# Gathered expert rows taken whole: 8 KB in one gather and one vector operation of 2048 columns

## What is computed

```python
q = (xb @ w_q).reshape(T, PEER_HEADS, 2, PEER_HALF)
sc = jnp.einsum('thcd,hckd->thck', q, sub_keys)
s1, i1 = lax.top_k(sc[:, :, 0], PEER_TOPK)
s2, i2 = lax.top_k(sc[:, :, 1], PEER_TOPK)
...
idx = e1 * PEER_N_KEYS + e2                 # 8 heads x 16 picks of 16384 experts
g = jax.nn.softmax(best.astype(jnp.float32), axis=-1)
u_sel = jnp.take(u_tab, idx, axis=0)        # rows of 2048
act = jax.nn.gelu(jnp.einsum('td,thkd->thk', xb, u_sel))
v_sel = jnp.take(v_tab, idx, axis=0)
return jnp.einsum('thk,thkd->td', g.astype(act.dtype) * act, v_sel)
```

## Time and profile before

| | |
|---|---|
| time, median of 3 runs | 1738.58 us (1735.13 to 1742.35) |
| time of the profiled execution | 1741.15 us |
| its span, first to last instruction | 1739.4 us |
| granted TensorE clock | 0.996 |
| busy: TensorE 1696.9, VectorE 1453.8, ScalarE 983.1, GpSimd 546.7 us | 98, 84, 57, 31% |
| moved by DMA | 496.67 MB |

### The profile page before, as it was taken

One profiled execution on the slowest core, in us unless ns is written; L12 is line 12 of the kernel. 1 busy time (PEld: TensorE's weight loads), 2 busy tenths in 40 slices (PEclk: granted clock), 3 DMA queues, 4 the chain that ended last, 5 costly groups with the idle time before them and its releaser, 6 DMA issues. The chain is left out here.

```text
span 1739.4 us, 28872 instructions
## 1 busy us (share of the span) xinstructions
PE 1696.9 (98%) x10918; PEld 1607.0 (92%) x10918; DVE 1453.8 (84%) x2071; ACT 983.1 (57%) x1590; POOL 546.7 (31%) x345
## 2 busy tenths in 40 slices
PE   9999999999999999999999999999999999999997
PEld 7887788878999999999999999999989999999887
DVE  4545776578899988888888999699889989999987
ACT  5544575453465667777775555655454555554454
POOL 0002310024222001101013445056655526585551
PEclk9999999999999999999999999999999999999999
DMA  7765445676677877777779999899999999999993
GB/s 233 218 182 167 147 146 171 194 252 205 206 231 231 274 238 254 241 244 233 247 228 354 375 378 385 257 332 395 371 378 393 390 332 389 406 393 408 403 397 143
DMA packets 136232, 496.67 MB, mean 286 GB/s; under 512 B 15632, under 2 KB 15792, under 8 KB 135392
## 3 DMA queue, kind: packets, MB, share of 16 engines
q1 hardware_dynamic: 95760, 347.65, 58.5%
q0 software_dynamic: 40048, 146.64, 22.8%
q10 hardware_dynamic: 288, 0.55, 0.1%
HBM read 489.44 MB, written 5.34 MB: 284 GB/s over the span
## 5 line engine op out<-in xcount | busy, mean ns | idle before, releaser
L776 ACT ACTIVATE HI<-V_RAW 128x1024 fp32r<-128x1024 f32 x256 | 271.7, 1062 | 286.1 <-DMA V_RAW<-peer_v 226.6
L1754 PE MATMUL PS<-W,HI 128*128 128x384 f32 x2048 | 413.7, 342 | 18.0 <-DVE W L1334 12.7
L1714 PE MATMUL PS<-xT,HI 128*128 128x384 f32 x2048 | 412.8, 343 | 1.9 <-ACT HI L776 1.3
L1754 PEld LDWEIGHTS PS<-W,HI 128*128 128x128 f32 x2048 | 348.7, 189 | 23.9 <-ACT HI L776 16.4
L1714 PEld LDWEIGHTS PS<-xT,HI 128*128 128x128 f32 x2048 | 347.4, 189 | 8.0 <-ACT HI L776 6.2
L541 POOL DMA_INDIRECT PICKED<-peer_u,PK x128 | 195.3, 1526 | 481.4 <-DVE DOTS L1315 460.6
L1250 DVE TENSOR_TENSOR V_LO<-V_RAW,HI 128x2048 fp32r<-128x2048 f32 x128 | 293.0, 2289 | 43.8 <-ACT HI L776 43.3
L776 ACT ACTIVATE HI<-RING_RAW 128x1024 fp32r<-128x1024 f32 x256 | 270.0, 1055 | 96.5 <-DMA RING_RAW<-u_t 92.2
L541 POOL DMA_INDIRECT PICKED<-peer_v,PK x128 | 241.0, 1883 | 212.9 <-DVE ACC L1323 108.9
L1257 DVE TENSOR_TENSOR RING_LO<-RING_RAW,HI 128x1024 fp32r<-128x1024 f32 x249 | 294.7, 1220 | 7.1 <-ACT HI L776 6.5
L1759 PEld LDWEIGHTS PS<-W,V_LO 128*128 128x128 f32 x2048 | 266.4, 191 | 0.1
(11 more groups left out here) (222 smaller groups left out, 1602.8 us busy)
## 6 DMA issues: line engine op xcount, KB each, us to landing
RING_RAW<-u_t SPq DMA_DIRECT2D x256, 512.0 KB, 4.9
V_RAW<-peer_v SPq DMA_DIRECT2D x256, 512.0 KB, 13.0
RAW<-w_in SPq DMA_DIRECT2D x80, 512.0 KB, 3.8
RAW<-w_out SPq DMA_DIRECT2D x32, 512.0 KB, 4.2
RAW<-wq_t SPq DMA_DIRECT2D x32, 512.0 KB, 4.9
x_spill<-X POOLq DMA_DIRECT2D x2, 1024.0 KB, 5.8
X<-xg_spill POOLq DMA_DIRECT2D x8, 256.0 KB, 7.4
PICKED<-peer_u,PK POOLq DMA_INDIRECT x128, 9.0
```

The source lines that it names most:

```text
L776: nc.scalar.activation(HI[:, n % HI_SLOTS, :], raw_of(n), ACT.Copy).then_inc(top_ready, 1)
L1714: return mm(PS[:, j % S_BANKS, 0:2 * ND].rearrange("p (a t) -> p a t", a=2), HI[:, n % HI_SLOTS, kk * P:(kk + 1) * P], xT[:, k, :, 0:ND], ...
L1754: return mm(PS[:, V_BANKS[i], 0:2 * ND].rearrange("p (a t) -> p a t", a=2), HI[:, v % HI_SLOTS, i * P:(i + 1) * P], weights_of(v), start=v ...
```

## The change

The half rows become whole rows. One gather fetches 8 KB into each partition, and one VectorE operation has 2048 columns. So there are 128 groups instead of 256. The buffers hold 8 KB a partition, three of them and from step 88 on four, where there were four and six of 4 KB. The list for the steps has 43 groups at other steps than before, that for the units 85 over the same 228 units. The sum of two half dots (L1328) and the two operations that made half-row indices are gone. The scratch for DMA descriptors is 4 KB a partition, not the default 16 KB, which moves every tile down and gives room for the third buffer.

```diff
-ROW_SLOTS, MORE_SLOTS = 4, 6
+ROW_SLOTS, MORE_SLOTS = 3, 4
...
-HALVES = 4 * NG
-HALF_STEPS = sorted([j for j in range(SPREAD0 - 3, SPREAD_END) if j % 5 % 2 == 0] + list(range(SPREAD_END, NKEYS - 7))
-                    + list(range(SPREAD_END, NKEYS - 7, 3)))
+N_ROWS = 2 * NG
+ROW_STEPS = ([j for j in range(SPREAD0 - 3, SPREAD_END) if j % 5 in (1, 3)]
+             + [j for j in range(SPREAD_END, NKEYS - 7) if j % 3])
...
-X8_AT = range(A_SUMS - 6 * ROWS_B, A_SUMS, 6)
+X8_AT = range(A_SUMS - 3 * ROWS_B, A_SUMS, 3)
...
-        PICKED = [at("PICKED0", 192 * KB, [P, HALF]), at("PICKED1", 196 * KB, [P, HALF]), at("PICKED2", 96 * KB, [P, HALF]),
-                  at("PICKED3", 100 * KB, [P, HALF]), at("PICKED4", 104 * KB, [P, HALF]), at("PICKED5", 108 * KB, [P, HALF])]
+        PICKED = [at("PICKED0", 192 * KB, [P, D]), at("PICKED1", 96 * KB, [P, D]), at("PICKED2", 208 * KB, [P, D]),
+                  at("PICKED3", 104 * KB, [P, D])]
...
-                pool.indirect_dma_start(PICKED[slot][:], None,
-                                        table.rearrange("e (a c) -> (e a) c", a=2),
-                                        bass.IndirectOffsetOnAxis(PK4[:, half, g:g + 1], 0))\
+                pool.indirect_dma_start(PICKED[slot][:], None, table, bass.IndirectOffsetOnAxis(PK4[:, 0, g:g + 1], 0))\
                     .then_inc(row_ready[slot], 16)
...
-                    ins = v.tensor_tensor_reduce(rows, rows, x_rows[0:np_, cols], 1.0, 0.0, ALU.mult, ALU.add,
-                                                 DOTS[0:np_, half, g:g + 1])
+                    ins = v.tensor_tensor_reduce(rows, rows, x_rows[0:np_, :], 1.0, 0.0, ALU.mult, ALU.add, DOTS[0:np_, g:g + 1])
...
-                        ins = v.scalar_tensor_tensor(acc, rows, DOTS[0:np_, 0, g:g + 1], acc, ALU.mult, ALU.add)
-                ins.then_inc(halves, 1)
+                        ins = v.scalar_tensor_tensor(acc, rows, DOTS[0:np_, g:g + 1], acc, ALU.mult, ALU.add)
+                ins.then_inc(rows_done, 1)
...
-    nc = bacc.Bacc("TRN2", target_bir_lowering=False, num_devices=1)
+    nc = bacc.Bacc("TRN2", target_bir_lowering=False, num_devices=1, dynamic_dma_scratch_size=4096)
```

More of the change, by code:

```diff
@@ L151, in ahead @@
     return 0 if j < ROWS_BACK_AT else ROW_SLOTS if j < MORE_AT else MORE_SLOTS
-GATHERED = {j: ahead(j) + sum(i < j for i in HALF_STEPS) for j in range(NKEYS)}
-MORE_FROM = ROW_SLOTS + sum(i < MORE_AT for i in HALF_STEPS)
+GATHERED = {j: ahead(j) + sum(i < j for i in ROW_STEPS) for j in range(NKEYS)}
+MORE_FROM = ROW_SLOTS + sum(i < MORE_AT for i in ROW_STEPS)
 def row_slot(k):
@@ L353, in hybrid_peer_block @@
         row_ready = [sem(f"row_ready{i}") for i in range(MORE_SLOTS)]
-        halves, dots, dots_gelu, sel_ready = sem("halves"), sem("dots"), sem("dots_gelu"), sem("sel_ready")
+        rows_done, dots_gelu, sel_ready = sem("rows_done"), sem("dots_gelu"), sem("sel_ready")
         w_hi, w_lo, half_done, flushed = sem("w_hi"), sem("w_lo"), sem("half_done"), sem("flushed")
@@ L530, in gather @@
             def gather(k):
-                dot, g, half = half_of(k)
+                dot, g = row_of(k)
                 table = peer_u if dot else peer_v
@@ L565, in _ @@
                     gather(k)
-            for k in range(GATHERED[NKEYS - 1], len(HALF_STEPS) + MORE_SLOTS):
+            for k in range(GATHERED[NKEYS - 1], len(ROW_STEPS) + MORE_SLOTS):
                 gather(k)
@@ L573, in _ @@
                      for c in range(D // BANK)]
-            for k in range(len(HALF_STEPS) + MORE_SLOTS, HALVES):
+            for k in range(len(ROW_STEPS) + MORE_SLOTS, N_ROWS):
                 gather(k)
@@ L578, in _ @@
                     pool.dma_start(X8[r * NB_:(r + 1) * NB_, :], xg_dram[NA:NS, :]).then_inc(x8_ready, 16)
-                if HALF_UNITS[k - MORE_SLOTS - len(HALF_STEPS)] >= NKEYS + 50 and late and k % 3 == 0:
+                if ROW_UNITS[k - MORE_SLOTS - len(ROW_STEPS)] >= NKEYS + 50 and late and k % 3:
                     pool.wait_ge(low_used, N_U + NKEYS + 44)
@@ L1294, in land, with full_rows @@
                 v.tensor_tensor(store[:, j, 0:t], store[:, j, 0:t], TMP[:, 0:t], ALU.mult).then_inc(landed, 1)
-            def half_rows(k):
-                dot, g, half = half_of(k)
-                cols = slice(half * HALF, (half + 1) * HALF)
+            def full_rows(k):
+                dot, g = row_of(k)
                 np_ = P if g < GROUPS_A else PB
@@ L1302, in half_rows @@
                 dve.wait_ge(row_ready[row_slot(k)], 16 * slot_count(k))
[L1303 removed]
+                gates = PK4[:, 1, :].bitcast(FP32)
                 if k in (A_DOTS, B_DOTS):
@@ L1360, in _ @@
                     land(j)
-                for k in range(len(HALF_STEPS)):
-                    if HALF_STEPS[k] == j:
-                        half_rows(k)
+                for k in range(len(ROW_STEPS)):
+                    if ROW_STEPS[k] == j:
+                        full_rows(k)
                 if j == FIRST_WEIGHTS_AT:
@@ L1814, in _ @@
                     pe.wait_ge(sel_ready, 2)
-                    pe.wait_ge(halves, A_SUMS)
+                    pe.wait_ge(rows_done, A_SUMS)
                     for i in range(DT):
```

61 lines of the change are left out of this document (27 added, 34 removed).

## The result

The changed kernel takes **1777.97 us** (median of 4 runs, 1768.96 to 1779.35) where the kernel before took 1738.96 beside it on the same chip: 1.0207 times as long, 95% interval 1.0178 to 1.0236. I forecast 1737 with a range to 1753. The forecast is wrong, on the side of rival C.

What follows compares the result with a forecast made beforehand. It took a VectorE-ScalarE ring to bound the spread, and VectorE and DMA at their limit the stage of values. From 1741.15 us, +13.9 and -15.5 gave 1739.6, less 2.6 to the median: 1737 us, range 1725 to 1753.

Steps and rivals of the forecast that it cites:

- rival C: After the spread: 8 KB gather packets take two bytes of three, loads land later than 8.1 us; 1770 us, chance 0.10.
- What bounds the kernel: Stage of values: TensorE loses 24.1 us, fed by VectorE and DMA at their limit; spread: VectorE and ScalarE set the pace.
- The ring of the spread: Spread: VectorE and ScalarE wait on each other in steps of 5.71 us, so VectorE delays beyond idle time reach the end.
- VectorE is a second limit in the stage of values: Stage of values, first stretch: VectorE, busy 178.8 of 195 us, is never free and limits beside the DMA supply.
- The spread, +13.9 us: Spread: 18 steps with a whole group of 2.21 us against 1.44 idle each lengthen 0.77 us; bounds 12 to 15.2.
- After the spread, "I take 0": From 910 to 1095 us: same bytes and rows as before, so no change, 2 us either way.
- The stage of values, -15.5 us: Stage of values: 7.5 us back in the first stretch by VectorE's 4.2%, 8.0 us later; bounds 7.2 to 24.1.
- The bigger packet itself no row shows ... and take 0: Stage of values: effect of larger gather packets on the rate taken as 0, bounded at 6 us either way.
- B: Stage of values: all 24.1 us lost there come back; 1728.4 us, chance 0.25.
- D: Spread: waits in the 18 longer steps lower TensorE's clock, 28 us more; 1765 us, chance 0.06.
- E: Spread's loss stands, stage of values returns under 5 us because supply dips set its pace; 1750 us, chance 0.09.
- Scratch, gathers' issue, the four loads of tokens B: Smaller scratch 0; half as many gathers from GpSimd, nobody waits behind it; four token loads queued behind gathers, 0.

Runs made afterwards that it cites:

- e7: Changed kernel's 2048-column operations only outside the spread, 1024 columns inside it at the steps of the kernel before, rows fetched by two 4 KB gathers; 1749.98 us.
- e2: Changed kernel's whole-row 8 KB gathers, buffers and scratch, but vector operations of 1024 columns at the steps and units of the kernel before; 1775.94 us.
- e1: Changed kernel, but each whole row fetched by two gathers of 4 KB a partition into the same 8 KB buffer; 1747.25 us.
- e9: Kernel before with 11 more half-row groups in the spread, leaving 169 for the stage of values; 1729.85 us.
- e11: Kernel before with a half-row group in every step to the spread's end, and stage-of-values loads from a copy with each unit's rows in order; 1717.53 us.
- e3: Kernel before with only the descriptor scratch cut to 4 KB; 1741.49 us, ratio 0.9998.

## Why the prediction was wrong, by its steps

- **What bounds the kernel.** The ring of the spread is right: its long steps got longer, and shorter operations took that back. That VectorE is a second limit in the stage of values: wrong. It was busy through its stretch and waited for hardly anything but `HI`, but e7 gave it 11 us of room (180 x 1.19 less 90 x 2.26) and that brought nothing. A VectorE that is late because its input is late can look full.
- **The spread, +13.9 us**: measured +14.8, and undone by shorter operations alone (e2, e7). The mechanism is right; that the sum agrees to 1 us is in part luck. The 18 steps gave 12.2 us, 0.68 each where 0.77 stood, at the lower bound. The idle time of 1.44 us counts from the end of the operation before, but the group starts 0.09 us before that end (798.21, where `land` ends at 798.30), so it has 1.53 us to fill. The other 2.6 us, from the spread's first step, were in no term. That step is 7.80 us, 6.67 in e1 and 5.39 in e2 and before: the long operation alone gives half of its growth, and the packets, which add nothing without it, the rest. By its own terms the upper bound is 15.1, not 15.2.
- **After the spread, "I take 0"**: measured +10.4. Failed. The bytes and rows are the same there; the size of their packets is not. With 4 KB packets it is +0.8 (e1), with 8 KB and short operations +7.7 (e2).
- **The stage of values, -15.5 us**: measured +10.6, the largest miss. Two parts are to be told apart. The relief itself exists, 11.9 us (e1), within the bounds of 7.2 to 24.1. Its cause is not the 4.2% of VectorE that I took for the first stretch but the bytes, which I had set at 4.9 us there and left aside: rows that are done in the scores need not be fetched here (e7 against e1, e9 against before).
- **"The bigger packet itself no row shows ... and take 0"**: this is the step that failed. It costs 22.5 us in the stage of values, beyond the bound of 6, and 9.6 us after the spread. I looked for what a packet does to the rate of the sum; what it does is to divide the rate otherwise. The mechanism stood in rival C.
- **Rival C (0.10)** had the mechanism, the point at which it decides (8.1 us; 8.3 measured) and 1770. It erred on where the loss lands: 18 us after the spread and nothing in the stage of values, because "with ten slots ... this is evened out before the next group". That would need 410 GB/s throughout; the loads alone get 256 to 265 in the mean, as rows from 1106 on could have told. That its 1770 came near 1778 is luck, since its two parts are not the measured ones. I had read the slices of full share and low rate (dips to 215 to 310 GB/s) as noise of the supply and not asked who was moving data in them.
- **Rivals B, D and E.** B: nothing of the 24.1 us came back in the changed kernel; it does in e11. D: the long steps didn't lower the clock, which is 1.00 in the mean from 640 to 930. It fell at the middle of the stage of values, to 0.76 for 21 us. E was right that the supply's dips set the pace of the stage, but gave 2 us back where 10.6 were lost.
- **Scratch, gathers' issue, the four loads of tokens B**: 0 for the scratch holds (e3); the others weren't tried alone.
- **Open.** Ahead of the spread the 8 KB kernels lose 2.1 to 3.0 us, the others up to 1.9; no run isolates it. Between the spread and the stage of values e7 takes 4.7 us more than before with packets of 4 KB, and e11 2.6 us more, which I can't explain. How much of the 10.4 us after the spread is the double share and how much a ring of six slots was not tried, since there was no room for more slots. Why loads of rows 1 MB apart are slow alone, and only after some 3 us of it, and not beside gathers, was not settled either.

## What to carry over

When two streams share the DMA engines, their packets' sizes divide the rate between them, as here by 107 packets of 8 KB to 109 of 4 KB. Making the burst stream's packets larger slowed the steady one, though the bytes stayed the same. Ask at what rate the steady stream catches up when it is alone; read that from a stretch where only it runs, and look at its rows' pitch first. And where an engine on the ring has 1.4 us idle a step, pieces of 1.1 us are nearly free (1.2 us for 11 more, 1.8 us for 21) and one of 2.3 us is not; fill the idle steps with small pieces and take them out of the stage that is short of supply.

## What the runs showed of the hardware

- Loads of 128 rows of 4 KB, 1 MB apart, alone from 1106 to 1114: 256 GB/s with the engines 93% busy; the same bytes with the rows one behind the other: 412 GB/s. Beside a queue of gathers the two together still came to 400 to 411 GB/s in most slices. Left alone after a burst of gathers, the loads kept some 400 GB/s for about 3 us and then fell to less than 230.
- Two queues with work get packets one for one: 107 of 8 KB against 109 of 4 KB in 3 us, 0.88 against 0.40 MB.
- Two indirect gathers of 2 KB a partition left no packet between 512 B and 2 KB in the records, and as many packets with rows as one of 4 KB. Each took GpSimd 1.5 to 1.7 us to issue in 1250 to 1400, where one of 4 KB took 1.5 to 1.9.
- Descriptor scratch of 4 KB against 16 KB: no effect (0.9998).
